# Attention by head pairs in two mixer stages of a hybrid encoder step on one Trainium2 core

## What is computed

```python
def stick_breaking(q, k, v, q_pos, k_pos):
    z = jnp.einsum('bqhd,bkhd->bhqk', q, k).astype(F32) * (q.shape[-1] ** -0.5)
    mask = k_pos[None, :] < q_pos[:, None]
    log_1mb = jnp.where(mask, jax.nn.log_sigmoid(-z), 0.0)
    later = lax.cumsum(log_1mb, axis=3, reverse=True) - log_1mb
    w = jnp.where(mask, jnp.exp(jax.nn.log_sigmoid(z) + later), 0.0)
    return jnp.einsum('bhqk,bkhd->bqhd', w, v.astype(F32))

def band_attend(q, k, v, q_pos, k_pos, bias_table):
    s = jnp.einsum('bqhd,bkhd->bhqk', q, k).astype(F32) * (q.shape[-1] ** -0.5)
    rel = jnp.clip(q_pos[:, None] - k_pos[None, :], -REL_CLIP, REL_CLIP) + REL_CLIP
    s = s + bias_table.astype(F32)[:, rel][None]
    ...
    p = jax.nn.softmax(jnp.where(mask, s, -1e30), axis=-1)
    return jnp.einsum('bhqk,bkhd->bqhd', p, v.astype(F32))
```

## Time and profile before

| | |
|---|---|
| runs | 2350.87, 2352.31, 2359.78 us; median 2352.31 |
| profiled execution | 2354.03 us, its span 2352.2 us |
| PE busy | 2275.0 us (97%) |
| DVE busy | 1106.0 us (47%) |
| ACT busy | 330.0 us (14%) |
| POOL busy | 1175.4 us (50%) |
| mean granted TensorE clock | 0.979 of full |

### The profile page before, as it was taken

How to read it: one execution, slowest core, us unless ns; L and a number is a source line. 1 busy time by engine, 2 the same in 40 slices (tenths; PEclk the granted TensorE clock), 3 DMA queues, 4 the chain that set the end, 5 groups by cost and what they waited for, 6 DMA issues and landing times.

```text
span 2352.2 us, 40834 instructions
## 1 busy us (share of the span) xinstructions
PE 2275.0 (97%) x17241; PEld 2190.3 (93%) x17241; DVE 1106.0 (47%) x1284; ACT 330.0 (14%) x498; POOL 1175.4 (50%) x646
## 2 busy tenths in 40 slices
PE   8999999999999999999999999999898989999997
PEld 7999999998778999999999999999886679999997
DVE  5441447354747441345644034647665464422433
ACT  2100000101561110000111000012203212100001
POOL 4565565543215565565565556545330145665563
PEclk9999999999999999999999999999998889999998
DMA  4222222221112221222222122222111022221221
GB/s 167 89 95 75 89 103 85 88 77 50 45 38 73 89 102 69 88 89 98 108 89 97 73 90 96 92 82 73 59 37 55 28 69 75 96 92 72 89 97 57
DMA packets 30169, 190.15 MB, mean 81 GB/s; under 512 B 3728, under 2 KB 4112, under 8 KB 11536
## 3 DMA queue, kind: packets, MB, share of 16 engines
q1 hardware_dynamic: 23904, 173.62, 20.6%
q10 hardware_dynamic: 6192, 15.51, 1.8%
HBM read 181.62 MB, written 7.50 MB: 80 GB/s over the span
## 4 chain that ended last, share of the span: by engine, by line
PE 91%; DVE 6%; issue 1%; ACT 1%; DMA 1%; POOL 1%; ACTq 0%; DVEq 0%; POOLq 0%
PE ps L415 74%; PE ps L428 7%; PE ps L964 1%; PE ps L1001 1%; PE ps L671 1%; DVE cacc L1774 1%; PE ps L738 1%; DVE rstd L1404 1%; PE ps L699 0%; DVE seg L1840 0%; PE ps L983 0%; PE ps L586 0%; POOL wl L387 0%; PE ps L702 0%; PE ps L606 0%
## 5 line engine op out<-in xcount | busy, mean ns | idle before, releaser
L415 PE MATMUL ps<-u,wh 128*128 128x272 f32 x6464 | 1084.8, 289 | 11.5 <-issue 5.6
L415 PEld LDWEIGHTS ps<-u,wh 128*128 128x128 f32 x6464 | 918.6, 188 | 13.8 <-issue 6.9
L384 POOL TENSOR_SCALAR wh<-wraw 128x1024 fp32r<-128x1024 f32 (+2 forms) x321 | 348.5, 1086 | 1122.0 <-PE ps L415 757.1
L387 POOL TENSOR_TENSOR wl<-wraw,wh 128x1024 fp32r<-128x1024 f32 (+2 forms) x321 | 826.8, 2576 | 26.8
L415 PE MATMUL ps<-u,wl 128*128 128x272 f32 x3232 | 669.7, 288 | 0.0
L415 PE MATMUL ps<-a,wh 128*128 128x272 f32 x3072 | 514.1, 289 | 1.1 <-issue 1.0
L415 PEld LDWEIGHTS ps<-u,wl 128*128 128x128 f32 x3232 | 506.4, 188 | 0.0
L415 PEld LDWEIGHTS ps<-a,wh 128*128 128x128 f32 x3072 | 435.9, 188 | 2.2 <-issue 1.6
L1429 DVE TENSOR_TENSOR tg<-ps,rstd 128x544 f32<-128x544 f32 x194 | 140.3, 725 | 593.2 <-PE ps L415 585.8
L415 PE MATMUL ps<-a,wl 128*128 128x272 f32 x1536 | 317.9, 288 | 0.0
L415 PEld LDWEIGHTS ps<-a,wl 128*128 128x128 f32 x1536 | 240.4, 188 | 0.0
(11 more groups left out here) (255 smaller groups left out, 1405.5 us busy)
## 6 DMA issues: line engine op xcount, KB each, us to landing
wraw<-in_wf_in SPq DMA_DIRECT2D x87, 1024.0 KB, 4.8
wraw<-in_wf_out SPq DMA_DIRECT2D x32, 1408.0 KB, 5.9
wraw<-in_w_ab SPq DMA_DIRECT2D x12, 1024.0 KB, 4.8
wraw<-in_w_cd SPq DMA_DIRECT2D x10, 1024.0 KB, 4.8
wraw<-in_w_abo SPq DMA_DIRECT2D x8, 512.0 KB, 3.3
wraw<-in_w_cdo SPq DMA_DIRECT2D x8, 512.0 KB, 3.3
out_y<-yout ACTq DMA_DIRECT2D x8, 272.0 KB, 2.1
bt<-in_bias ACTq DMA_DIRECT2D x1, 2048.0 KB, 8.6
```

The lines of the kernel that those rows point to most:

```text
L384: nc.gpsimd.tensor_scalar(wh[:, s, 0:K * P], raw, 1.0, 1.0, ALU.mult, ALU.mult).then_inc(w_high, 1)
L387: nc.gpsimd.tensor_tensor(wl[:, s, 0:K * P], raw, wh[:, s, 0:K * P].bitcast(F32), ALU.subtract).then_inc(w_split[s], 1)
L415: last = nc.tensor.matmul(bank(b0 + 2 * s + half, 0, HT), w[:, s, k * P:(k + 1) * P], act_t[:, k0 + k, part, half * HT:(half + 1) * HT], s ...
```

## The change

In layer 0: the state matmuls alternate between the two heads of a pair; `cr` is rounded earlier on DVE; `part(6, 1)` and `part(7, 0)` move ahead of a `ret_norm` each; the mask is added with the scores, so that DVE no longer zeroes anything; there are four weight buffers `se` in place of three, and `stick_out` does two heads at a time, alternating between output rows 0 to 63 and 64 to 127.

In layer 1: `part(1)` goes to bank 4 and does not wait for bank 0; every half from there on stands one place later in the state-space tiles, and `part(23)` follows the squares. The band goes in 17 steps of one head pair and tile (the sample of all heads is one step, before the last pair). The scores of the pair's heads use rows 0 to 63 and 64 to 127 of the array and two banks. The row sum is divided out before the transposes (`band_scale`), and the values are now the stationary operand, so the output comes out with features on the partitions and nothing is transposed back. Each step but the first has one `ssd_product` half. The weights of queries and keys are interleaved, and the sample's bias comes as an input of its own. Cut to its core:

```diff
-        PRODUCT_AT = [8 + 2 * j for j in range(2 * DC)]
-        BACK_AT = [14, 24, 34, 42]
-        BACK_OUT = [sum(p_ <= n for p_ in PRODUCT_AT) for n in BACK_AT]
-        BACK_BEFORE = {q: 2 * c + 2 for c, q in enumerate(BACK_OUT)}
+        BAND = [(c, t) for c in range(3) for t in range(TILES)] + [(3, TILES)] + [(3, t) for t in range(TILES)]
+        BAND_N = len(BAND)
+        FIRST_OUT = [p_ - 1 for p_ in range(BAND_N)]
...
                 pe.wait_ge(ro_root, 1)
+                for c in range(2):
+                    for j in range(TILES):
+                        for h in (2 * c, 2 * c + 1):
+                            b = 64 * (h % 2)
+                            nc.tensor.matmul(bank(5, c * P, (c + 1) * P, b, b + 64), kd[:, j, h * 64:(h + 1) * 64],
+                                             rv_n[:, j, h * P:(h + 1) * P], start=(j == 0), stop=(j == TILES - 1),
+                                             skip_group_check=True)
                 for h in range(RET_H):
                     c, b = h // 2, 64 * (h % 2)
-                    for j in range(TILES):
-                        nc.tensor.matmul(bank(5, c * P, (c + 1) * P, b, b + 64), kd[:, j, h * 64:(h + 1) * 64],
-                                         rv_n[:, j, h * P:(h + 1) * P], start=(j == 0), stop=(j == TILES - 1),
-                                         skip_group_check=True)
                     last = nc.tensor.matmul(bank(5, 256 + c * P, 256 + (c + 1) * P, b, b + 64),
                                             kd[0:LS, 4, h * 64:(h + 1) * 64],
...
+                    for j in range(TILES):
+                        last = nc.tensor.matmul(psf[:, B + OFF[j]:B + OFF[j] + P], cr[:, CR_ID, :],
+                                                cr[:, CR_MASK, :], start=False, stop=False, skip_group_check=True)
...
-                        last = nc.tensor.matmul(psf[:, o:o + P], cr[:, CR_ID, :], cr[:, CR_MASK, :], start=False,
-                                                stop=True, skip_group_check=True)
...
+            def stick_out(p_, before):
+
+                two = (p_ - 1, p_)
                 pe.wait_ge(sb_w, p_ + 1)
...
+                for j in range(TILES):
+                    for q in two:
+                        h = HEADS[q]
+                        b = 64 * (h % 2)
                         last = nc.tensor.matmul(bank(6, j * P, 512, b, b + 64),
-                                                sv_n[:, j, h * 64:(h + 1) * 64], W[:, OFF[j]:OFF[j] + LEN[j]],
+                                                sv_n[:, j, h * 64:(h + 1) * 64],
+                                                se[q % 4][:, OFF[j]:OFF[j] + LEN[j]],
                                                 start=(j == 0), stop=(j == TILES - 1))
-                else:
-                    for hh in range(SB_H):
-                        c, b = hh // 2, 64 * (hh % 2)
-                        for kt in range(3):
-                            n = P if kt < 2 else LS
+                last.then_inc(so_done, 1)
...
+                if p_ == 2:
+                    stick_out(1, 0)
+                elif p_ == 4:
+                    stick_out(3, 1)
+                elif p_ == 5:
+                    stick_out_sample(4, 2)
+                elif p_ == 7:
+                    stick_out(6, 3)
...
+                if n == 0:
+                    pe.wait_ge(evac[0], c0 + 4)
+                elif n == 2:
+                    pe.wait_ge(half_free, HALVES_AB + 1)
+                elif half and m:
                     pe.wait_ge(half_free, HALVES_AB + m + 1)
-                elif m == 0:
-                    pe.wait_ge(evac[0], c0 + 4)
-                else:
+                elif m:
                     s_, q_ = chunks[m - 1]
                     pe.wait_ge(evac[s_], (c0, c1)[s_] + q_ + 1)
-                half_product(s, (c0, c1)[s] + p_, DC, u, half, 0)
+                half_product(s, (c0, c1)[s] + p_, DC, u, half, 4 if n == 1 else 0)
...
+                c, t = BAND[n]
+                B = 2 + 2 * (n % 2)
+                if n >= 2:
...
+                    for e in range(2):
+                        r = slice(64 * e, 64 * e + 64)
+                        last = nc.tensor.matmul(bank(B + e, 0, w), bq_t[r, c, t * P:(t + 1) * P], bk_t[r, c, 0:w],
+                                                start=True, stop=True)
...
+                c, t = BAND[n]
+                pe.wait_ge(b_norm, n + 1)
+                if n:
+                    pe.wait_ge(bp_copied, n)
+                else:
+                    pe.wait_ge(y_root, 1)
+                p_ = pr[n % 2]
+                for e in range(2):
+                    if t < TILES:
+                        for j in range(t + 1):
+                            last = nc.tensor.transpose(bank(6 + e, j * P, (j + 1) * P), p_[:, e, j * P:(j + 1) * P],
...
-                        last = nc.tensor.matmul(bank(6 + n % 2, 0, 64, 0, LS), pt_[0:m, j * LS:(j + 1) * LS], v,
-                                                start=(j == 0), stop=(j == 2))
+                        for e in range(2):
+                            h, b = 2 * c + e, 64 * e
+                            last = nc.tensor.matmul(bank(1, t * P, (t + 1) * P, b, b + 64),
+                                                    bv_n[:, j, h * 64:(h + 1) * 64], pt[:, e, j * P:(j + 1) * P],
+                                                    start=(j == 0), stop=(j == t), skip_group_check=True)
...
-                    band_back(BACK_AT.index(n))
+            for n in range(BAND_N):
+                band_turn(n)
+                if n:
+                    ssd_product(FIRST_OUT[n])
+                if n + 2 < BAND_N:
+                    band_s(n + 2)
+                band_out(n)
...
+                c, t = BAND[n]
                 act.wait_ge(bp_done, n + 1)
-                if n >= 2:
-                    act.wait_ge(bo_done, n - 1)
+                if n:
+                    act.wait_ge(bo_done, n)
+                else:
+                    act.wait_ge(y_done, 5)
...
+                    nc.scalar.copy(pt[:, :, 0:w], ps[:, 6:8, 0:w]).then_inc(bp_copied, 1)
...
-                V.tensor_tensor(d, d, strict.unsqueeze(1).broadcast_to([P, 3, P]), ALU.mult)
-                d = S[:, OFF[3]:OFF[3] + P]
-                link(V.tensor_tensor(d, d, strict, ALU.mult))
...
             ret_att(2)
             part(3, 1)
+            dve.wait_ge(rg_ready, 4)
+            for to, at_ in ((CR_NEGT, C_NEGT), (CR_NEG1, C_NEG1), (CR_ID, C_ID), (CR_MASK, C_MASKNEG)):
+                V.tensor_scalar(cr[:, to, :], C(at_), 1.0, None, ALU.mult).then_inc(cr_ready, 1)
...
             ret_norm(1)
             part(6, 0)
+            part(6, 1)
             ret_norm(2)
-            part(6, 1)
+            part(7, 0)
             ret_norm(3)
-            part(7, 0)
             part(7, 1)
...
+                    dve.wait_ge(bp_done, n - 1)
+                w = (t + 1) * P if t < TILES else PAST + LS
+                for e in range(2):
+                    bias = bt[:, 2 * c + e, (3 - t) * P:512] if t < TILES else bsm[:, e, :]
+                    V.tensor_tensor_reduce(pr[n % 2][:, e, 0:w], bank(B + e, 0, w), bias, -1.0, 3e38,
+                                           ALU.add, ALU.min, bst[:, n % 2, 0, e:e + 1]).then_inc(b_max, 1)
+
+            def band_scale(n):
+
+                c, t = BAND[n]
+                w = (t + 1) * P if t < TILES else PAST + LS
+                b = bst[:, n % 2, :, :]
+                dve.wait_ge(b_exp, 2 * n + 2)
+                link(V.reciprocal(b[:, 2, :], b[:, 1, :]))
+                for e in range(2):
+                    p_ = pr[n % 2][:, e, 0:w]
+                    last = V.tensor_scalar(p_, p_, b[:, 2, e:e + 1], None, ALU.mult)
+                last.then_inc(b_norm, 1)
...
+            band_max(0)
+            band_max(1)
+            part_evac(23)
+            ssd_inverse()
+            band_scale(0)
+            ssd_scale(0)
+            ssd_scale(1)
+            for n in range(BAND_N):
+                if n + 1 < BAND_N:
+                    band_scale(n + 1)
+                if n == 0:
+                    ssd_scale(2)
+                    ssd_scale(3)
+                if n:
+                    ssd_add(FIRST_OUT[n])
+                if n + 2 < BAND_N:
+                    if BAND[n + 2][1] == TILES:
+                        dve.wait_ge(cdc_loaded, 64)
+                    band_max(n + 2)
+                if n == 4:
+                    for i in range(2):
+                        r = slice(64 * i, 64 * i + 64)
+                        last = V.tensor_copy(bqz[r, :, i, :], bq_t[r, :, LP:T])
+                    last.then_inc(bq_ready, 1)
+                if BAND[n][1] >= TILES - 1:
+                    band_mix_(n)
             residual(CD_OUT, 1.0, 5, 2)
```

More of the change, by code:

```diff
@@ L746, in stick_out, with stick_out_sample @@
+            def stick_out_sample(p_, before):
+                W = se[p_ % 4]
+                pe.wait_ge(sb_w, p_ + 1)
+                pe.wait_ge(so_mix, before)
```

(6 more changed lines are left out.)

386 lines of the change are left out of this document (157 added, 229 removed).

## The result

The changed kernel takes 2263.19 us (median of four runs, 2262.03 to 2264.75) against 2354.62 us for the kernel before on the same chip: a ratio of 0.9611, with a 95% interval of 0.9596 to 0.9626. The forecast was 2288 us with a range of 2268 to 2316. The profiled execution took 2262.03 us, with a span of 2260.2 us.

A forecast was written before the change was run, and what follows sets the result against it. TensorE (PE) was taken to set the time, through matmuls, waits for DVE or ACT, and low clock. Savings of 13.3 + 12.3 + 37.4 + 1.7 = 64.7 us gave 2288 us, range 2268 to 2316.

The forecast's parts named there:

- The way the halves work: Layer 0 stick-breaking outputs: two heads alternating in 64-column halves run in parallel, saving 7.5 us.
- with the second overlapping half of the first 4.0 us: Band scores of a head pair over four tiles: 4.0 us with half overlap, against 5.06 us serially.
- The sample's output: Layer 0, 4.89 us before: fewer changes of array form, 16 before and 8 after, save 0.7 us.
- The retention state: Layer 0: 32 records go from 0.117 to 0.066 us each and six form changes go, saving 2.1 us.
- Of the 7 us I take 4: Layer 0 near 591 us: moving roundings and evacuations on DVE removes 4 us of a wait and low clock.
- the 1 us I charged: Layer 0: shorter outputs bring PE sooner to the next head's ACT and DVE chain, costing 1 us.
- the sum of 9.0 us: Layer 1 before the band: 5.6 us wait, 2.7 us low clock of part(1), 0.7 us shorter queue saved.
- 11.9 us in the opening: Band opening: PE waits 4.8, 3.4 and 3.7 us for DVE's reciprocal and scalings, plus 5 us low clock.
- I charge 2 us a pair: Band steps: waits for the softmax chain and POOL-slowed DVE, on top of 15.6 us work, giving 17.6 us.
- Halves in turn: Rival for layer 0 and the band: halves run one after the other, saving 48.2 us, 2304 us; chance 0.34.
- The clock with half of the array at work: Rival: half-array work lowers PE's clock from the mark on, 65 us more, 2353 us; chance 0.05.
- The chain per step: Rival in the band: each step's operations follow serially, 36.7 us a pair, 2372 us; chance 0.04.

The follow-up runs named there:

- e2: Changed kernel with the two heads of a stick-breaking output in turn instead of alternating: 2268.54 us, ratio 0.9652.
- e3: Changed kernel with the first head's band scores before a step's half product and the second head's behind it: 2278.15 us, ratio 0.9683.
- e4: Changed kernel with DVE's old order around the first stick-breaking scores (four roundings, part(6, 1) and part(7, 0) later again): 2269.13 us, ratio 0.9648.
- second trace of the change: The changed kernel run once more, unaltered, on another chip's rounds: 2262.4 us, ratio 0.9608.
- e5: Changed kernel with part(1) back in bank 0, where it waits for the evacuation of part(0): 2267.81 us, ratio 0.9615.
- e1: Changed kernel with a band step's output matmuls in turn, all of the first head and then all of the second: 2267.59 us, ratio 0.9635.
- b1: Changed kernel with DVE's reciprocal ahead of the last evacuation, part_evac(23), at the opening of the band: 2262.89 us, ratio 0.9597.

## Why the prediction was right and where it wasn't

**The way the halves work** was right, its size in part. "If they run side by side, 2.30 us plus the record by which the second head starts later, so 2.73 us": the second head starts 6 ns later, not a record, and the pair takes 2.30 us. That is 9.2 for 7.5 us, shown by the records and by e2. The same step priced the scores: "with the second overlapping half of the first 4.0 us" is 2.95 us, all of it overlapped (e3). The sample's output takes 2.35 us in place of the 4.2 I left it (saved 2.5, not 0.7), since I counted only its changes of form and let its records run in turn. The retention state takes 2.5 in place of 5.5 us, 3.0 for 2.1.

**The gap in layer 0.** "Of the 7 us I take 4": it was 7.8 (from the start of the last two halves to the first scores 6.5 in place of 14.3 us), and e4 brings all of it back. I expected that DVE would only be late at another place; in the first trace it isn't, in the second by 2.4 us. Against that the heads lost more than the 1 us I charged. The records save 9.2 + 2.5 = 11.7 us from the first scores on, the stage only 7.6, so 4.1 are lost. PE waits there for ACT, and two stretches (623 to 631 and 671 to 679 us) have the low clock, of which I had let only the later one stand. In the second trace of the change the waits for ACT are 4.3 us and the second of these stretches isn't there, and the stage takes 116.3 us; how the loss divides between the two isn't fixed. Waits between 580 and 705 us, and one of the stretches:

```profile
PE ps L675 <- ACT se L1245: 2.5, 3, 1.3
```

```profile
623.00:631.00 8.00, 8.00 (x32) 6.71 (x31) 1.21 (x2) 4.55 (x4) 0.00 (x0) 0.57 0.01 2
```

**Before the band** the sum of 9.0 us for `part(0)` to `part(2)` was right: from the first half product to the first `ssd_out` it is 32.9 before and 20.0 after, 12.9 with the moved half of 3.3, so 9.6. Its parts were not: I gave the bank the whole wait and low clock, 8.3 us, and e5 shows 5.4. What I missed is the tiles, 3.6 us. I read of the earlier trace rows only the wait before `part(1)` and didn't ask what each moved half does to GpSimd's start. The last 1.5 us of the 18.0 lie nearly all in stages that aren't touched, and are scatter.

**The band** holds two thirds of the error, 17.3 us, and here two terms of the sum were mis-sized. The larger one is PE's waits. I put them at 11.9 us in the opening, 2 us a pair and 2 us for DMA issues, together 21.9; PE is idle for 9.2 us in the opening and 1.0 in the steps, together 10.2, which is 11.7 us less. The smaller one is the work of a pair: 15.6 us were forecast and 14.55 measured, four times 1.05 us. It is made up, by the distance between starts, of the scores (2.95 us for 4.0), the outputs (2.8 for 3.0), the transposes (2.1 for 2.4) and the products (6.7 for 6.2). So the step that failed is the price of a pair, "I charge 2 us a pair" for waits on top of 15.6 us of work. From product to product a pair takes 14.5 us (1758.65 to 1773.18 us) and the next one, which holds the one longer wait, 15.5, against 17.6.

The three waits of the opening are 4.7, 1.7 and 2.8 us, where I had 4.8, 3.4 and 3.7. The low clock lasts until 1757.5 us, as I thought, but behind the opening it costs some 2.2 us (5.1 us at 0.56) of the 5 I charged; the rest of it lies beside DVE's work.

The chain shows the place that I feared, the maximum, exponentials and copy of tile 3 ahead of the outputs of tile 2, and between them something that I had priced by itself:

```profile
1771.87 0.69 DVE pr L1941
1772.61 0.72 ACT pr L1338
1773.42 0.61 ACT pr L1338
1774.13 0.43 ACTq L1369
1774.60 0.47 ACTq L1369
1775.16 0.81 ACT pt L1350
1776.01 0.88 PE ps L1031 x12
```

It is 4.1 us long and PE waits 0.9 us of it. L1369 are DMA issues on ACT's queue (`bk_t` to its output), 0.9 us that the copy stands behind. In the last pair the same place has no issue and takes 3.0 us, and PE waits 0.15 us; those are all the waits in the steps. So the softmax chain alone is shorter than the 3.6 to 4.3 us of the forecast and nearly hidden by PE's work, and the wait that there is comes with the DMA issues: 0.9 us where I had 2.

What the 54.7 us of this stage are made of is shown in part only. e1 and e3 take back 3.0 and 13.7 us. PE is idle for 16.5 us of it before and 10.2 after. By the clock of the windows before (0.76 from 1763.67 to 1794 us, 0.84 from there to 1905.5) and after (0.81 and 0.96), some 25 and 7 us are lost to the low clock, an estimate that counts idle time too. The new place of the operands, the end of `band_back` and the steps of a pair were not taken back one by one.

**The rivals.** Halves in turn: e1, e2 and e3 show what that would cost, at least 20 us, and that it isn't so. (Two numbers of this rival don't follow from their terms: in layer 0 they give 0.3 + 0.7 + 0.5 + 4 = 5.5 us before the charge of 1, not 5.9, and in the band 4 x (1.06 + 1.7) = 11.0 us over the 104.5, not 9.1. It would have stood at 2306 or 2307 us, which changes nothing here.) The clock with half of the array at work: 1.00 in the steps, so out. The chain per step: waits of 0.9 and 0.15 us in all, so out. The range was too narrow on its low side because the unknown prices were leaned to the dear end together: 4 of 7, a whole record of delay, half of an overlap, 2 us a pair. Its low end allowed for the waits in the steps and the gap, but not for the cheaper work of a pair (4.2 us), nor for the sample's output, or the tiles, at all.

## What to carry to other kernels

Where float32 matmuls use half of the columns or half of the rows, issue the two halves alternately: here the second was then free (2.30 us for one head and for two), and in turn it was paid for except at the seam (3.86 us). When the overlap of alternating halves is forecast, price it as complete or absent and keep both; half of an overlap was wrong here in either case. Look also at what the queue of an engine off the critical path issues between two links of a chain: the one longer wait in the steps came from there. Of a moved step ask also when it frees a buffer, since that sets when GpSimd runs, and whether VectorE then reads two SBUF operands beside it.

## What the runs showed that I hadn't expected

- Two float32 matmuls in different halves start and end 6 ns apart, for column halves (128*64, L741, L1031) and for row halves (64*128, L985). In turn, the second half's records begin beside the fourth from last of the first.
- A DVE multiplication of 0.68 us takes 2.88 us beside a GpSimd subtraction, and PE's next half product then starts 1.5 us late.
- The low clock after the opening (0.56 and 0.58 granted) lasted 5.1 us in the change, 3.0 us in b1 and 13.4 us in e3, with PE busy throughout.
